# One TensorE reordering in the expert stage, a reload in halves, and new orders around it, in a three-block transformer kernel

## The reference

```python
q, kv, k_rope                    # "mla": 8 heads of softmax attention
mq, mk, mv, ig, fg               # "ml": 4 heads of a gated linear attention
ml_out = (norm(hm) * g + skip * xc) * silu(z)
x = x + concatenate([attn_out, ml_out]) @ w_o             # 1024 x 1024
# mixture of experts: 32 experts in 4 groups, 2 chosen for each token
y_e = (silu(h @ w_gate_e[e]) * (h @ w_up_e[e])) @ w_down_e[e]
x = x + sum of weight * y_e                               # 3 MB of weights per expert
x = x + (p @ w_ple) * sigmoid(rmsnorm(x) @ w_ple_gate)
return rmsnorm(x, final_norm)
```

## Time and profile before

| | us |
|---|---|
| median of 3 runs | 1007.81 |
| lowest, highest | 1006.74, 1008.88 |
| the profiled execution's own time | 1010.66 |
| its span from first to last instruction | 1009.0 |
| TensorE busy / VectorE / ScalarE | 952.6 / 635.9 / 533.6 |
| HBM read | 222.50 MB |

### The profile page before, as it was taken

One profiled execution on the slowest core, in us unless ns is written; L12 is line 12 of the kernel. 1 busy time (PEld: TensorE's weight loads), 2 busy tenths in 40 slices (PEclk: granted clock), 3 DMA queues, 4 the chain that ended last, 5 costly groups with the idle time before them and its releaser, 6 DMA issues.

```text
span 1009.0 us, 14997 instructions
## 1 busy us (share of the span) xinstructions
PE 952.6 (94%) x5635; PEld 731.1 (72%) x5635; DVE 635.9 (63%) x1392; ACT 533.6 (53%) x973; POOL 84.1 (8%) x97
## 2 busy tenths in 40 slices
PE   6999899999999999999999999999899999987786
PEld 5777588888888877688888888868676665443345
DVE  4679768999845566768999845666876221110046
ACT  6657767666635565767666635765852211100054
POOL 0100001121100301001121101010000000000000
PEclk9999999999999999999999999999999999999998
DMA  8934246656565544256655664314578999999971
GB/s 273 386 129 126 84 151 196 197 167 204 198 190 185 186 162 129 84 151 195 197 167 205 198 177 148 135 48 168 212 312 311 399 405 420 421 421 421 421 280 44
DMA packets 99359, 224.58 MB, mean 223 GB/s; under 512 B 9535, under 2 KB 64210, under 8 KB 86994
## 3 DMA queue, kind: packets, MB, share of 16 engines
q1 hardware_dynamic: 99122, 223.04, 61.7%
q10 hardware_dynamic: 160, 0.53, 0.1%
HBM read 222.50 MB, written 1.05 MB: 222 GB/s over the span
## 4 chain that ended last, share of the span: by engine, by line
PE 75%; DMA 10%; DVE 8%; ACT 3%; SPq 2%; issue 1%; DVEq 0%; ACTq 0%
PE ps L559 72%; DMA ringx<-in_w_up_e_dram 5%; PE ps L563 3%; DMA xs<-in_w_down_e_dram 3%; DVE wl L1991 2%; SPq L3002 1%; DVE smb L2005 1%; DMA ring<-in_w_uv_dram 1%; SPq L3005 1%; DMA ring<-in_w_in_even_dram 1%; ACT wh L1446 1%; ACT L1443 1%; ACT pb L1443 0%; ACT hh L1443 0%; DVE x L1991 0%
## 5 line engine op out<-in xcount | busy, mean ns | idle before, releaser
L1991 DVE TENSOR_TENSOR wl<-ring,wh 128x1024 fp32r<-128x1024 f32 (+3 forms) x212 | 268.9, 1270 | 105.4 <-ACT wh L1446 104.1
L1446 ACT ACTIVATE wh<-ring 128x1024 fp32r<-128x1024 f32 (+3 forms) x212 | 222.2, 1051 | 105.2 <-PE ps L559 101.3
L559 PE MATMUL ps<-hx,wh 128*128 128x512 f32 (+1 forms) x720 | 245.0, 387 | 0.1
L559 PE MATMUL ps<-hx,wl 128*128 128x256 f32 x704 | 196.6, 280 | 0.0
L559 PEld LDWEIGHTS ps<-hx,wh 128*128 128x128 f32 x720 | 133.7, 187 | 28.8 <-issue 0.6
L559 PEld LDWEIGHTS ps<-hx,wl 128*128 128x128 f32 x704 | 133.1, 189 | 0.0
L559 PE MATMUL ps<-ring,xg 128*32 128x256 f32 (+1 forms) x592 | 78.0, 381 | 7.4 <-DMA ring<-in_w_up_e_dram 4.7
L2947 POOL TENSOR_TENSOR fs<-fs,rt 128x256 f32<-128x256 f32 x44 | 52.5, 1213 | 355.5 <-ACT fs L1443 355.5
L559 PE MATMUL ps<-wh,hh 128*128 128x512 f32 (+3 forms) x192 | 78.9, 411 | 3.4 <-DVE wl L1991 3.2
L559 PE MATMUL ps<-wl,hh 128*128 128x512 f32 (+3 forms) x192 | 74.2, 386 | 0.0
L559 PE MATMUL ps<-wh,hl 128*128 128x512 f32 (+3 forms) x192 | 72.9, 387 | 0.0
(11 more groups left out here) (317 smaller groups left out, 1673.7 us busy)
## 6 DMA issues: line engine op xcount, KB each, us to landing
ring<-in_w_up_dram SPq DMA_DIRECT2D x88, 512.0 KB, 4.7
ring<-in_w_down_dram SPq DMA_DIRECT2D x22, 1024.0 KB, 5.0
ring<-in_w_up_e_dram SPq DMA_DIRECT2D x19, 1024.0 KB, 18.8
ring<-in_w_gate_e_dram SPq DMA_DIRECT2D x18, 1024.0 KB, 13.3
ring<-in_w_down_e_dram SPq DMA_DIRECT2D x15, 1024.0 KB, 26.0
ringx<-in_w_down_e_dram SPq DMA_DIRECT2D x14, 1024.0 KB, 21.4
ring<-in_w_in_odd_dram SPq DMA_DIRECT2D x12, 1024.0 KB, 5.1
ringx<-in_w_gate_e_dram SPq DMA_DIRECT2D x12, 1024.0 KB, 16.5
```

The costliest lines, as they stand in the source:

```text
L559: return e.matmul(o, l, r, start=start, stop=stop)
L1446: return e.activation(o, i, ACT.Copy)
L1991: return e.tensor_tensor(o, a, b, op)
```

## The change

TensorE, in the stages around the experts:

```diff
@@ router
...
             for t in range(2):
+                if t == 1:
+                    embed(0, 0)
                 for k in range(8):
...
-            for t, n in ((0, 0), (0, 1), (1, 0)):
+            for t, n in ((0, 1), (1, 0)):
                 embed(t, n)
@@ gate_up: gate (g = 0) and up (g = 1) can be asked for apart
-            def gate_up(i):
-                b, n = take("gu", i), P // len(members[i])
-                for g in range(2):
+            def gate_up(i, gs):
+                if 0 in gs:
+                    take("gu", i)
+                b, n = bank[use["gu", i][0]], P // len(members[i])
+                for g in gs:
...
+                            if i == 0 and g == 0 and k == 4:
+                                gu.inc(w, i)
+                                half_done[u_gu[0, 0]] = (gu.sem, gu.n)
@@ down
-                bs = [take("dn", i, n) for n in range(2)]
+                bs = [claim(n, "dn", i, n) if i == 0 else take("dn", i, n) for n in range(2)]
@@ order of the expert stage
-            for i in range(10):
-                gate_up(i)
+            gate_up(0, (0, 1))
+            gate_up(1, (0,))
+            act_T(0)
+            gather(1, 0)
+            down(0)
+            for i in range(1, 10):
+                gate_up(i, (1,) if i == 1 else (0, 1))
...
-                if i >= 1:
-                    scatter(i - 1)
+                scatter(i - 1)
```

The load order and SP; `parts` are now two halves of the down weight of expert 5, and the definition of `embed` moved up as it was:

```diff
+            if u == u_dn[NS - 1]:
+                order = order[:4] + order[6:8] + order[4:6] + order[8:]
...
+                (view, src), = parts
+                parts = [(lambda v, f=view, j=j: f(v)[:, j:j + 1, :], src[:, j:j + 1, :]) for j in range(2)]
@@ sync
+                if u == u_dn[NS - 1]:
+                    q.wait_ge(s_sort, 1)
+                    for n in (NS, NS + 1):
+                        found[n] = e.value_load(ids[0:1, n - NS:n - NS + 1], min_val=0, max_val=NE - NS - 1)
+                    for done, (view, src) in zip((half_done, unit_done), parts):
+                        q.wait_ge(*done[before[u]])
+                        e.dma_start(view(slot[k]), src).then_inc(loaded[k], 16)
+                    continue
```

ScalarE, before and in the loop, where `out_at[2]` is steps 11 to 14 and the four products of `hm` at step 13 stay (VectorE's `fa`, `ysl` and sorting of the expert stage are untouched):

```diff
-            swish(0)
             for i in (1, 3):
                 evac(flat(qT3[0:96, 2 * i:2 * i + 2, :]), "q2T", i, rows=96)
+            swish(0)
@@ i == 11
                     copy(mix[:, 1, 512:1024], b[:, :]).then_inc(of(drained, "ml", 1), 1)
+                    for m in range(4):
+                        emptied(q, "z", m)
+                    act(szT[:, :, :], szT[:, :, :], ACT.Silu).then_inc(s_sz, 1)
+                if i == 12:
+                    next(outp)
+                if i == 13:
+                    warm()
+                    mix_hi("mla", 1, mla_hi[:, 1, :])
+                    q.wait_ge(s_var, RV["mln"])
+                    act(st[:, 16:24], st[:, 8:16], ACT.Sqrt).then_inc(s_std, 1)
                     q.wait_ge(s_xc, 2)
                     for h in range(4):
                         act(xcT[:, h, :], xcT[:, h, :], ACT.Copy, scale=gain("sk2", h))
-                if i == 12:
-                    for m in range(4):
-                        emptied(q, "z", m)
-                    act(szT[:, :, :], szT[:, :, :], ACT.Silu).then_inc(s_sz, 1)
-                    warm()
-                if i == 13:
-                    q.wait_ge(s_var, RV["mln"])
-                    act(st[:, 16:24], st[:, 8:16], ACT.Sqrt).then_inc(s_std, 1)
-                if i in out_at[2]:
                     next(outp)
                 if i == 13:
                     q.wait_ge(s_hsb, 1)
...
-            mix_hi("mla", 1, mla_hi[:, 1, :])
+                if i == 14:
+                    next(outp)
+            next(outp)
@@ expert step 0: the copy of aT before the gather's copies
-                if i < 8:
+                if 0 < i < 8:
                     gather(i // 2 + 1, i % 2)
...
+                if i == 0:
+                    gather(1, 0)
```

VectorE, in the loop (at step 11 `next(hms)` now stands before the split of that step) and behind it, where `split_lo(c_outm + 5)` is the `wl` of chunk 4 and `g` counts the two halves of the `ml` result:

```diff
+                if i == 11:
+                    next(hms)
+                if i == 2:
+                    next(proj)
+                    next(proj)
...
+                if i == 13:
+                    mix_lo("mla", 1, mla_hi[:, 1, :], mla_lo[:, 1, :], 10)
                     next(hms)
-                if i == 14:
-                    mix_lo("mla", 1, mla_hi[:, 1, :], mla_lo[:, 1, :], 10)
                 if i == 0:
-                    next(proj)
-                    next(proj)
                     gate_rows(0)
@@ behind the loop; g counts the two halves of the ml result
-            split_lo(c_outm + 5, wh, wl)
...
+                if g == 0:
+                    split_lo(c_outm + 5, wh, wl)
                 split_lo(c_outm + 6 + g, wh, wl)
```

The end. Square of row block 0 is taken in two halves, the first as soon as its half is ready. The sigmoids of the last two quarters and their gated additions are cut into two parts of 256 columns. The two half sums of a norm are joined in one instruction (`second_root`) instead of an addition and a scaling. Of the last 1024 columns ScalarE scales the first 512 from a product made earlier, VectorE the other 512:

```diff
+                own.inc(tt(sg[:, 1, 0:512], x[:, 1, 0:512], gfl[:, 0:512], ALU.mult))
...
-                for n in range(2):
-                    last(1, n, 512)
+                second_root("fin1", st[:, 2:3], st[:, 4:5], st[:, 25:26])
+                stt(xs[:, 1, 512:1024], x[:, 1, 512:1024], st[:, 25:26], gfl[:, 512:1024], ALU.mult, ALU.mult).then_inc(s_xn, 1)
@@ ScalarE
+                q.wait_ge(s_rstd, RV["fin1"])
+                act(xs[:, 1, 0:512], sg[:, 1, 0:512], ACT.Copy, scale=st[:, 25:26]).then_inc(s_xna, 1)
```

More of the change, by code:

```diff
@@ L297, in build @@
         place, in_slot, landed = {}, [None] * (XS + 1), [0] * (XS + 1)
-        before = {}
+        before, half_done = {}, {}
         order = list(range(NU))
@@ L1250, in tensor @@
             norm_T("nf2", added((2, "out")))
[L1251 to L1258, removed]
             up = unit_in(q, u_ple).rearrange("p (k n) -> p k n", k=2)
@@ L1265, in embed @@
                 w.then_inc(of(full, "ple", t, n), 1)
-            for t, n in ((0, 0), (0, 1), (1, 0)):
+            q.wait_ge(s_ur, 32)
+            b = take("route")
+            for t in range(2):
+                if t == 1:
+                    embed(0, 0)
+                for k in range(8):
+                    if t == 0 and k % 2 == 0:
+                        emptied(q, "nf2", k // 2)
+                    w = mm(b[:, t * 36:(t + 1) * 36], hT[:, k, t * P:(t + 1) * P], ur[:, k, :], k == 0, k == 7)
+            w.then_inc(of(full, "route"), 1)
+            for t, n in ((0, 1), (1, 0)):
                 embed(t, n)
@@ L2881, in tail, with gated @@
                 rinv("np2", 2, DM, rin[:, 14:16])
-                def gated(t, n):
-                    c = slice(n * 512, (n + 1) * 512)
-                    emptied(q, ("gate", n), t)
-                    emptied(q, "ple", t, n)
-                    own.inc(tt(sg[:, t, c], sg[:, t, c], ple[:, t, c], ALU.mult))
-                    tt(x[:, t, c], x[:, t, c], sg[:, t, c], ALU.add).then_inc(s_sgm, 1)
+                def gated(t, c0, c1, upto):
+                    q.wait_ge(s_sg, upto)
+                    own.inc(tt(sg[:, t, c0:c1], sg[:, t, c0:c1], ple[:, t, c0:c1], ALU.mult))
+                    tt(x[:, t, c0:c1], x[:, t, c0:c1], sg[:, t, c0:c1], ALU.add).then_inc(s_sgm, 1)
@@ L2890, in half @@
                 def half(n):
                     c = slice(n * 512, (n + 1) * 512)
[L2893 removed]
+                    q.wait_ge(s_sgm, (2, 6)[n])
                     own.inc(ttr(xs[:, 1, c], x[:, 1, c], x[:, 1, c], ALU.mult, ALU.add, 0.0, st[:, 1 + n:2 + n]))
[L2896 to L2898 removed]
@@ L2900, in tail, with second_root @@
-                q.wait_ge(s_gf, 16)
-                for t, n in ((0, 0), (1, 0), (0, 1)):
-                    gated(t, n)
+                def second_root(name, total, part, o):
+                    stt(st[:, 8:9], total, 1.0 / DM, part, ALU.mult, ALU.add).then_inc(s_var, 1)
+                    q.wait_ge(s_std, RV[name])
+                    rcp(o, st[:, 16:17]).then_inc(s_rstd, 1)
+                    q.wait_ge(s_rstd, RV[name])
+                q.wait_ge(s_gf, 16)
+                for t, n in product(range(2), range(2)):
+                    emptied(q, "ple", t, n)
@@ L2903, in tail @@
+                gated(0, 0, 512, 1)
+                gated(1, 0, 512, 2)
+                gated(0, 512, 768, 3)
+                gated(0, 768, 1024, 4)
                 half(0)
+                own.inc(ts(st[:, 4:5], st[:, 1:2], 1.0 / DM, EPS, ALU.mult, ALU.add))
+                own.inc(tt(sg[:, 1, 0:512], x[:, 1, 0:512], gfl[:, 0:512], ALU.mult))
+                q.wait_ge(s_sqh, 1)
+                own.inc(ts(st[:, 5:6], st[:, 3:4], 1.0 / DM, EPS, ALU.mult, ALU.add))
                 q.wait_ge(s_sq, SQ["fin0"])
-                rinv("fin0", 1, DM, st[:, 24:25])
@@ L2906, in tail @@
-                last(0, 0, DM)
-                gated(1, 1)
+                second_root("fin0", st[:, 0:1], st[:, 5:6], st[:, 24:25])
+                stt(xs[:, 0, :], x[:, 0, :], st[:, 24:25], gfl[:, :], ALU.mult, ALU.mult).then_inc(s_xn, 1)
+                gated(1, 512, 768, 5)
+                gated(1, 768, 1024, 6)
                 half(1)
-                own.inc(tt(st[:, 0:1], st[:, 1:2], st[:, 2:3], ALU.add))
-                rinv("fin1", 1, DM, st[:, 25:26])
```

(7 more changed lines are left out.)

41 lines of the change are left out of this document (23 added, 18 removed).

## The result

The changed kernel took 1013.06 us (median of 6, 1012.02 to 1019.04), the kernel before 1007.9 beside it (6 runs): a ratio of 1.0054, interval 1.0039 to 1.0070, so about 5.4 us slower. Timed again with the experiments, 11 runs against 34, it was 1.0038 (1.0026 to 1.0050), 3.8 us. The forecast was +2.7 with a range up to 1013.4: the sign and the order of waits hold, the size is half of the first ratio and 0.7 of the second.

A forecast was written before the change was run, and what follows sets the result against it. It took the weight stream behind 789 us, started by the end of `down(1)`, as the bound. -2.85 + 0.35 + 0.85 + 0.4 + 3.6 + 1.15 - 0.8 = +2.7 on 1007.81 gave 1010.5 us, range 1006.6 to 1013.4.

The forecast's parts named there:

- What the time hangs on: Expert stage: when TensorE ends `down(1)` frees the slot for expert 11's gate weight and so starts the remaining weight stream.
- The loop: Attention loop: `ml` head 1 at 681.0 and head 2 at 686.8 instead of 689.65, -2.85 us, bounds -1.6 and -3.5.
- The projection, its order: Output projection: value product loses its 2.87 us wait, but chunk 4 waits 2.85 for its `wl`; +0.35 us.
- The projection's clock: Output projection: TensorE's clock may fall behind the wait at chunk 4; +0.85 us, bounds 0 and 1.7.
- The router: Router: logits one embed later, so TensorE's rank product waits for VectorE's mask; +0.4 us, bounds 0 and 1.
- The expert stage's wait: Expert stage: TensorE stands still 4.7 us for `fa` and starts the gather of step 1 later; +3.6 us.
- the chain: Expert stage: gather needs the bank `fa` 1 frees; `fa` 1 follows the sorting, which follows `ysl` and `down(0)`: 783.5 us.
- Its clock: Expert stage: TensorE's clock falls behind the 4.7 us wait; +1.15 us, bounds 0 and 1.7.
- The end: Last scaling split over two engines and one VectorE addition less; -0.8 us, bounds -0.4 and -1.2.
- the loop gives less, the clocks cost all: Rival: attention loop gains only 1.6 us and both clock falls cost fully; +5.3, 1013.1 us, chance 0.10.

The follow-up runs named there:

- gates back: Changed kernel with the expert stage's order as before, gate products of step 1 behind the down products of step 0: 0.9999 of the kernel before.
- gates and split back: Changed kernel with the expert stage's old order and chunk 4 of the output projection split where it was: 0.9974 of the kernel before.
- loads back: Changed kernel with other gather banks, earlier sorting and chunk 4's old split place, but expert loads as in the kernel before: 0.9957 of the kernel before.
- sorting: Changed kernel with VectorE's sorting and its tables moved ahead of its part of the gather of step 0, banks unchanged: 0.9977 of the kernel before.
- the first profile: First profiled execution of the kernel before, unedited: 1010.66 us, 2.85 above the median of its three runs.
- banks: Changed kernel with both gathers of the second group of steps in banks 2 and 3 instead of the rotation's: 1.0009 of the kernel before.
- the second profile of the kernel before: The kernel before profiled once more, unedited; 31.2 us from the first gate product to the load of expert 11's gate weight.
- filled wait: Changed kernel with 38 small TensorE products put in the wait ahead of the gather of step 1: 1.0015 of the kernel before.
- the run with ScalarE's queue: Changed kernel with other gather banks, earlier sorting and chunk 4's old split place, ScalarE issuing the store of its scaled half: 0.9955 of the kernel before.
- the split back: Changed kernel with VectorE splitting its half of chunk 4 ahead of the products with hmT, as before; as the only edit 1.0020 of the kernel before.

## Why the forecast had the sign and half the size

**What the time hangs on: right, as long as the stream runs short there.** The end of `down(1)` sets the load of `xs` and that load the rest. Over the thirteen profiles of the usual clock it is issued between 784.4 and 794.4 us, and from it to the end of the span lie 216.9 to 220.3 us. A part of those 3.4 us of spread fits the stream: in three kernels (gates back, gates and split back, loads back) it was still full at that load, and there it is 219.2 to 219.5. The 219.2 of "sorting" and the 220.3 of the first profile (0.86 of it its wait) are not explained; there the stream did dip.

**The loop: right.** `ml` head 1 at 680.98 (forecast 681.0), head 2 at 686.69, so -2.96 for -2.85. The profile names no releaser for the 0.35 us ahead of head 2 ("issue"); VectorE's last read of the bank ended 0.1 us before it, as the forecast had it.

**The projection, its order: right.** The value product comes at 712.38, in the time of before 715.3. ScalarE's and VectorE's timelines answer: the table load, the products of `hm`; then the `wl` of chunk 3, the product with silu(z), and the `wl` of chunks 4 and 5 as one group:

```profile
712.25 1.28 ACT L1462 ACT_TABLE_LOAD   x1
...
716.40 1.65 ACT L1462 ACTIVATE xs<-xs,smb 128x128 f32<-128x128 f32 x4 [0.43 <-DVE smb L2033]
```

```profile
719.03 1.23 DVE L2023 TENSOR_TENSOR wl<-ring,wh 128x1024 fp32r<-128x1024 f32 x1 [1.51 <-ACT wh L1465]
720.17 1.22 DVE L2023 TENSOR_TENSOR sA<-sA 128x1024 f32<-128x1024 f32 x1
...
724.79 2.35 DVE L2023 TENSOR_TENSOR wl<-ring,wh 128x1024 fp32r<-128x1024 f32 x2
```

Chunk 4 starts at 726.06, 2.67 earlier, so +0.29 on the loop's gain for +0.35. The wait is 2.74 for 2.85. The next ScalarE instruction, at 713.54, stands 1.29 behind the start of the table load. So the 2.66 us of the Trainium skill (ScalarE: Activation LUTs, What ACT_TABLE_LOAD costs) are not seen here either.

**The projection's clock: the step that failed.** "I take half of 1.7, +0.85, as the earlier waits of this stretch may draw the low time into an idle one." They did not. Chunk 4 to the transposes took 12.6 for 10.9 us, 1.75, my upper bound, in four of the six profiles with that wait; 3.0 in one and nothing in another. The changed kernel's typical price is the whole, not the half.

**The router: right.** From the transposes to the rank 11.53 for 11.11 us, +0.42 for +0.4.

**The expert stage's wait: right.** Idle for 4.71 us (forecast 4.7), the gather 3.46 later counted from gate 0 (forecast 3.6), by the bank, the sorting and `down(0)` as the chain had it; "banks" and "sorting" show the first two links, each by itself.

**Its clock: the step that failed most.** "Part of the low stretch may lie inside the wait, where it costs nothing: bounds 0 and 1.7, taken 1.15." From the gather to gate 2 it took 11.25 for 8.58 us, 2.67, over the upper bound. The bound came from the earlier trace rows, where the low level lasted 3.4 us, and the second profile of the kernel before shows that it lasts 7 as well. The "filled wait" took it away alone and gave 2.7. The Trainium skill (TensorE: Matmul & The Clock Gate, HAM oscillation) warned of waits for a DMA that are followed by slow matmuls, and charges half the slow time; the wait here is for VectorE. Of the 6.9 us of low clock 0.8 lay in the wait, and half of the other 6.1 is 3.0, against 2.67 measured: the trace agrees within 0.4, and my bound had been taken from too short a stretch.

**The end: over-sized, by a term left out.** -0.8 taken, with -0.4 as the bound. From the last group of matmuls to the end of the span it is 10.8 in both profiles of before and 10.5 on the mean of the eleven that have the new end (10.2 to 10.7): -0.3. VectorE gains more than I took: it ends 6.9 us behind the start of that group for 8.0, so -1.1. But the stretch from VectorE's end to the span's end grew by 0.8. VectorE ends at 1008.63 and the span at 1012.4, 3.8 later, where the earlier trace rows end at 1006.13 and the span at 1009.0, 2.9 later; over all eleven it is 3.3 to 3.9 (mean 3.6), in the two profiles of before 2.9 and 2.8. Before, the first half's store was on its way while the second was scaled; now both come due at once. That this is the reason is argued and not shown; the run with ScalarE's queue shows only that it is not SyncE's issuing one behind the other. I had named no price for the stores.

**The sum again**, with what was measured: -2.96 + 0.29 + 1.75 + 0.42 + 0.1 (rank to gate 0) + 3.46 + 2.67 - 0.3 = +5.4, against +5.4 and +3.8 by the two ratios. The terms come from single profiles, and which of the two ratios is nearer stays open. Of the missing 2.7, 2.4 are clock and 0.5 the end. The rival nearest to this was "the loop gives less, the clocks cost all", 1013.1 with a chance of 0.10: the time fits, the loop half of it does not.

## What to carry to other kernels

Before an order is changed on the engine that leads, list which bank of the rotation each later product takes and which instruction of another engine frees it. Here a block of VectorE work of 6 us stood in front of the one small instruction (`fa`) that TensorE needed. The same engine stood still for 3.8 us a little earlier, and with the block there TensorE waited for nothing. A long wait of TensorE (here 2.7 us and more) is to be priced twice, as time and as clock, and the clock's price is to be taken whole and as a spread, from several executions. And whether a load that is issued earlier can help hangs on whether the stream runs short at that place: compare what the DMA engines move there before and after. Where two engines share a last step, ask what their stores do when they come due together.

## What the runs showed that I had not expected

The clock's fall is not a property of the wait alone. Ahead of chunk 4 six profiles of the usual clock have a wait of 2.7 us: it cost nothing once, 1.75 four times and 3.0 once. Behind the wait of 4.71 the clock was low for 3.4 us in one execution and 7 in another. The 1.6 us ahead of chunk 4 in the five kernels with the split back were followed by no fall, though 1.05 us of waiting stand some 4 us before them, and neither was a single wait of 1.16 (sorting). 1.81 with 0.48 behind it was, and so were the two of 1.02 and 1.10 us in the loop of the kernel before, in both its profiles. So neither the longest wait nor the sum of those near each other sorts these cases. And one execution ran at a granted clock of 0.95, not at either level, in windows as short as 0.1 us, from 12 us on except where it fell lower, with the kernel the same and the two long waits nearly so (2.74 and 4.57 for 2.74 and 4.71). It took 6 us more than the median of its kernel. Why is not known.
